# RMS norms of a two-block transformer kernel: sums in four column groups of 128 tokens, root and reciprocal on 128 columns, spread back by a one-row selector product

## The reference, cut to what matters

```python
def rms_norm(x, g):
    xf = x.astype(jnp.float32)
    y = xf * lax.rsqrt(jnp.mean(xf * xf, axis=-1, keepdims=True) + EPS)
    return (y * g.astype(jnp.float32)).astype(x.dtype)
```

## Time and profile before

| | before |
|---|---|
| median of 3 runs | 3803.28 us |
| the profiled execution | 3806.89 us |
| its span in the trace | 3805.1 us |
| mean granted TensorE clock | 0.903 of 2.4 GHz |
| PE busy | 3185.7 us (84%) |
| DVE busy | 1077.3 us (28%) |
| ACT busy | 647.6 us (17%) |

### The profile page before, as it was taken

How to read it: one execution, slowest core, us unless ns; L and a number is a source line. 1 busy time by engine, 2 the same in 40 slices (tenths; PEclk the granted TensorE clock), 3 DMA queues, 4 the chain that set the end, 5 groups by cost and what they waited for, 6 DMA issues and landing times.

```text
span 3805.1 us, 44308 instructions
## 1 busy us (share of the span) xinstructions
PE 3185.7 (84%) x18944; PEld 1617.3 (43%) x18944; DVE 1077.3 (28%) x2009; ACT 647.6 (17%) x1340; POOL 194.5 (5%) x180
## 2 busy tenths in 40 slices
PE   6896679999788888999999976728899989989873
PEld 3552234444333444566666654413344433333331
DVE  3341330000422121145555554331112111111114
ACT  0131100000001222234433442000111101101100
POOL 0000000000000000011111111020000000000001
PEclk9996789999897888999999996759999999999986
DMA  3114212212100000411111100065777899999993
GB/s 144 45 56 174 103 44 78 76 56 88 47 31 18 18 28 28 160 39 44 51 39 39 39 34 2 9 222 234 311 305 314 360 404 379 386 395 385 398 375 149
DMA packets 119322, 581.11 MB, mean 153 GB/s; under 512 B 12806, under 2 KB 24086, under 8 KB 72534
## 3 DMA queue, kind: packets, MB, share of 16 engines
q1 hardware_dynamic: 92274, 531.69, 35.6%
q10 hardware_dynamic: 20436, 24.26, 1.8%
q0 software_dynamic: 6416, 22.32, 1.6%
HBM read 549.76 MB, written 28.47 MB: 152 GB/s over the span
## 4 chain that ended last, share of the span: by engine, by line
PE 73%; DMA 12%; DVE 9%; ACT 3%; issue 2%; POOL 1%; SPq 0%; DVEq 0%; POOLq 0%; ACTq 0%
PE product_banks L768 35%; PE product_banks L1011 12%; DMA space<-in_wgu 8%; PE product_banks L1033 7%; PE score_banks L814 4%; PE score_banks L942 3%; PE turn_bank L799 3%; PE out_bank L836 2%; DVE rstd L1340 1%; DMA space<-in_wt 1%; PE turn_bank L827 1%; PE product_banks L755 1%; DMA y_rows<-zeros 1%; PE turn_bank L1022 1%; DVE space L1544 1%
## 5 line engine op out<-in xcount | busy, mean ns | idle before, releaser
L768 PE MATMUL product_banks<-space 128*128 128x512 f32 (+3 forms) x4064 | 1453.5, 511 | 56.4 <-DVE space L1471 15.3
L768 PEld LDWEIGHTS product_banks<-space 128*128 128x128 f32 (+1 forms) x4064 | 711.5, 193 | 711.5 <-issue 621.3
L1011 PE MATMUL product_banks<-space 128*32 128x512 f32 x5440 | 630.0, 608 | 64.0 <-DMA space<-in_wgu 62.5
L1011 PEld LDWEIGHTS product_banks<-space 128*32 128x32 f32 x5440 | 180.0, 111 | 451.7 <-issue 327.9
L1033 PE MATMUL product_banks<-space,rstd 128*32 128x256 f32 x5440 | 332.3, 399 | 46.4 <-ACT rstd L1275 30.3
L1663 DVE TENSOR_TENSOR sq<-product_banks,space 128x512 f32<-128x512 f32 x85 | 58.8, 692 | 758.4 <-PE product_banks L1011 758.4
L1033 PEld LDWEIGHTS product_banks<-space,rstd 128*32 128x32 f32 x5440 | 207.0, 115 | 152.6 <-issue 83.5
L1118 ACT ACTIVATE space<-product_banks 128x512 f32<-128x512 f32 (+2 forms) x238 | 113.0, 526 | 881.9 <-PE product_banks L768 879.0
L814 PE MATMUL score_banks<-space 64*128 64x256 f32 (+5 forms) x352 | 173.6, 598 | 34.9 <-ACT space L1132 17.9
L799 PE MATMUL turn_bank<-sq,cst 128*128 128x512 f32 (+1 forms) x196 | 107.0, 685 | 112.3 <-DVE sq L1336 112.0
L684 POOL TENSOR_TENSOR space<-space 128x512 f32<-128x512 f32 x112 | 133.8, 1209 | 1180.0 <-ACT space L1214 1087.4
(11 more groups left out here) (241 smaller groups left out, 2154.6 us busy)
## 6 DMA issues: line engine op xcount, KB each, us to landing
space<-in_wgu SPq DMA_DIRECT2D x256, 1024.0 KB, 13.9
space<-in_wdn SPq DMA_DIRECT2D x128, 1024.0 KB, 20.7
space<-in_wt SPq DMA_DIRECT2D x104, 1024.0 KB, 5.4
y_rows<-zeros ACTq DMA_DIRECT2D x2, 6400.0 KB, 27.7
y_rows<-zeros ACTq DMA_DIRECT2D x85, 128.0 KB
space<-in_wt SPq DMA_DIRECT2D x12, 512.0 KB, 4.3
space<-in_wt SPq DMA_DIRECT2D x8, 576.0 KB, 3.8
x<-in_xT SPq DMA_DIRECT2D x1, 2048.0 KB, 15.8
```

Of the source, the lines that this page charges most:

```text
L768: ins = nc.tensor.matmul(bank[0:rows, at:at + cols], lhsT, rhs, start=(i == 0), stop=(i == len(mm) - 1))
L1011: ins = nc.tensor.matmul(bank[ROWS * g:ROWS * g + ROWS, :], xT_[:, k, :], w[:, 512 * g:512 * g + 512], start=(k == 0), stop=(k == DC - 1))
```

## The change

Sums: a chunk's 512 columns are taken as four quarters of 128 tokens, and quarter q is multiplied by 32 columns of ones into PSUM partitions 32q to 32q+31, columns 0 to 127. One 128x512 product becomes four of 32x128 in four column groups of the array. Root: ACT reads the sums straight from PSUM, 128 columns on all partitions, and takes scale and epsilon with it (a new constant `eps`). DVE's mean-plus-epsilon instruction is gone, and its reciprocal is on 128 columns. Spreading: a new PE piece, `norm_spread`, multiplies `rstd` by a matrix that picks row 32q (a column of the identity, broadcast), once for each quarter, and writes the 512 values on all partitions into the PSUM bank `out_bank` (`PO`). The applications read them there. Norms of 256 columns do the same with 64.

```diff
+                    for q in range(4):
+                        ins = nc.tensor.matmul(PT[ROWS * q:ROWS * q + ROWS, 0:w // 4], ones[:, 0:ROWS], sq[:, g % 2, w // 4 * q:w // 4 * (q + 1)],
+                                               start=(c == 0), stop=(c == nch - 1))
+                    ins.then_inc(s_mm, 1)
...
+            def norm_spread(name):
+
+                n = NI[name]
+                w = NORMS[n][3]
+                pe.wait_ge(s_inv, n + 1)
+                for q in range(4):
+                    ins = nc.tensor.matmul(PO[:, w // 4 * q:w // 4 * (q + 1)], ident[:, ROWS * q:ROWS * q + 1].broadcast_to([P, P]),
+                                           rstd[:, 0:w // 4], start=True, stop=True)
+                ins.then_inc(s_rs, 1)
...
             norm("pre_mix")
+            norm_spread("pre_mix")
             norm("mem")
+            norm_spread("mem")
             pe.wait_ge(s_norm, normed("pre_mix", 1))
             products("in1", "pre_mix")
...
                 for d in range(2):
                     fill(2 * d)
-
+                    if n and d == 0:
+                        norm_spread(f"head{n - 1}")
                     pe.wait_ge(s_kd, 2 * n + d + 1)
...
                 norm(f"head{n}")
+            norm_spread("head7")
...
-                act.wait_ge(s_ms, n + 1)
-                nc.scalar.activation(ms[:, 0:w], ms[:, 0:w], F.Sqrt).then_inc(s_rt, 1)
+                _, _, nch, w = NORMS[n]
+                act.wait_ge(s_mm, chunk0[n] + nch)
+                nc.scalar.activation(ms[:, 0:w // 4], PT[:, 0:w // 4], F.Sqrt, bias=const("eps"), scale=1.0 / (P * nch)).then_inc(s_rt, 1)
...
-                dve.wait_ge(s_mm, chunk0[n] + nch)
-                V.tensor_scalar(ms[:, 0:w], PT[:, 0:w], 1.0 / (P * nch), EPS, ALU.mult, ALU.add).then_inc(s_ms, 1)
                 dve.wait_ge(s_rt, n + 1)
-                link(V.reciprocal(rstd[:, 0:w], ms[:, 0:w]))
+                V.reciprocal(rstd[:, 0:w // 4], ms[:, 0:w // 4]).then_inc(s_inv, 1)
+                dve.wait_ge(s_rs, n + 1)
...
-                link(V.scalar_tensor_tensor(osb, osb, vcol("hg_norm_g_2"), rstd[:, :], ALU.mult, ALU.mult))
+                link(V.scalar_tensor_tensor(osb, osb, vcol("hg_norm_g_2"), PO[:, :], ALU.mult, ALU.mult))
```

More of the change, by code:

```diff
@@ L59 @@
           ("more_no", N_MORE), ("token_no", TT), ("group_of", P), ("tie", N_EXP), ("rank_at", N_EXP), ("row_at", N_EXP),
-          ("room_at", N_EXP)]
+          ("room_at", N_EXP), ("eps", 1)]
 CONST_AT = {}
@@ L288, in build @@
         s_mm = sem("squares_summed")
-        s_ms = sem("mean_squares_ready")
         s_rt = sem("roots_ready")
+        s_inv = sem("inverse_roots_ready")
+        s_rs = sem("inverse_roots_spread")
         s_norm = sem("norm_written")
@@ L798, in norm @@
                     pe.wait_ge(s_sq, g + 1)
-                    nc.tensor.matmul(PT[:, 0:w], ones, sq[:, g % 2, 0:w], start=(c == 0), stop=(c == nch - 1)).then_inc(s_mm, 1)
+                    for q in range(4):
[10 more added lines that the diff above has]
+                ins.then_inc(s_rs, 1)
             def rope(r):
@@ L870, in _ @@
             norm("attn")
+            norm_spread("attn")
             norm("conv")
+            norm_spread("conv")
             norm("xattn")
+            norm_spread("xattn")
             pe.wait_ge(s_norm, normed("xattn"))
@@ L875, in _ @@
             norm("post_mix")
+            norm_spread("post_mix")
             norm("pre_mlp")
+            norm_spread("pre_mlp")
             pe.wait_ge(s_norm, normed("pre_mlp", 1))
@@ L881, in _ @@
             norm("post_mlp")
+            norm_spread("post_mlp")
             if stop == "x1":
@@ L884, in _ @@
             norm("mix2")
+            norm_spread("mix2")
             pe.wait_ge(s_norm, normed("mix2", 1))
@@ L887, in _ @@
             norm("ctx")
+            norm_spread("ctx")
             pe.wait_ge(s_norm, normed("ctx"))
@@ L890, in _ @@
             norm("qin")
+            norm_spread("qin")
             norm("ckv_lat")
+            norm_spread("ckv_lat")
             norm("ckv_ctx")
+            norm_spread("ckv_ctx")
             pe.wait_ge(s_evac, stages["in2"][1])
@@ L962, in _ @@
             norm("ffn2")
+            norm_spread("ffn2")
             pe.wait_ge(s_norm, normed("ffn2"))
@@ L1093, in _ @@
             norm("final")
+            norm_spread("final")
         @block.scalar
@@ L1344, in norm_apply @@
                 for c in range(nch):
-                    V.scalar_tensor_tensor(dst[:, c, 0:w], src[:, c, 0:w], gain(c), rstd[:, 0:w], ALU.mult,
+                    V.scalar_tensor_tensor(dst[:, c, 0:w], src[:, c, 0:w], gain(c), PO[:, 0:w], ALU.mult,
                                            ALU.mult).then_inc(s_norm, 1)
@@ L1446, in add_normed @@
                 for c in range(nch):
-                    link(V.scalar_tensor_tensor(src[:, c, :], src[:, c, :], gain(c), rstd[:, :], ALU.mult, ALU.mult))
+                    link(V.scalar_tensor_tensor(src[:, c, :], src[:, c, :], gain(c), PO[:, :], ALU.mult, ALU.mult))
                     link(V.tensor_tensor(x[:, c, :], x[:, c, :], src[:, c, :], ALU.add))
@@ L1780, in constants @@
     put("room_at", np.array([ROWS * n for n in BLOCKS_AT] + [0])[None, :])
+    put("eps", EPS)
     put("token_no", (np.arange(P)[:, None] + P * np.arange(TT)[None, :]))
```

3 lines of the change are left out of this document (1 added, 2 removed).

## The result

The changed kernel takes 3864.71 us (median of 4 runs, 3861.95 to 3873.74) against 3803.78 (4 runs): a ratio of 1.0165, with a 95% interval of 1.0153 to 1.0178. It is 1.6% slower. The profiled execution took 3861.95 us, its span is 3859.9 against 3805.1, its mean granted clock 0.895 against 0.903.

The account below looks back on a forecast made before the run. PE was taken to bound most of the span, plus norms where everything waits. 3806.89 + 120 (heads) - 57 (norms) = 3870 us for a profiled execution, 3.6 above the median, so 3866; range 3840 to 3892, 8 in 10 within 3830 to 3900.

Parts of the forecast that it names:

- DVE waits for a spreading that stands behind the fill, and PE for DVE: Passages into heads 1 to 6: PE's turns start 17.2 us later a head, 103 us in all, bounds 96 to 109.
- The clock after the wait: Heads, after PE's wait: work restarts at the lower clock, losing 2.8 us a head, 17 for six, bounds 0 to 27.
- The eight heads together: Head norms: stall and clock add 120 us for heads 0 to 5; ends of heads 6 and 7 save 4.3.
- The fifteen norms by themselves: Norms with no other work beside them: quicker sums, root and reciprocal save time, within a 57 us total including heads 6 and 7.
- Applications from PSUM at nothing: DVE's applications in the norms: reading the factor from PSUM costs nothing, gain or loss up to 0.05 us each.
- Up to four times for four column tiles: Norm sums on PE: the skill's rule would make a chunk some 0.2 us, not 0.46, the sum about 4 us better.
- The drain at a change of mode: Heads, PE switching between projections and sums: the skill's rule says each tiling switch drains the engine; no size was given.
- the clock stays low: Rival, chance 0.10: in the heads, slow work after each stall costs 10 us a head instead of 2.8; 3909 us.
- The wait is not on PE's path: Rival, chance 0.05: spreading gets ahead of the fill or DVE's 15.97 us is covered; only norms' gain stays, 3746 us.

Follow-up runs that it names:

- e3: Changed kernel with each head's spreading moved on PE from behind all 26 products of the fill to behind the first 4; 3748.77 us, ratio 0.9861.
- e4: Changed kernel plus 16 constant products on PE between the spreading and the turns in heads 1 to 6; 3843.37 us, ratio 1.0109.
- e1: Kernel before, with the new norm in the eight head norms only and the fifteen others old; 3925.13 us, ratio 1.0323.
- e2: Kernel before, with the new norm in the fifteen standalone norms only and the eight head norms old; 3740.08 us, ratio 0.9839.
- e6: Changed kernel with each head's spreading placed on PE ahead of all 26 products of the fill; 3771.56 us, ratio 0.9921.
- e8: e2 plus constant products on PE behind a norm's last chunk and between norms, none between chunks; 3728.48 us, ratio 0.9803.
- e7: e2 plus constant products on PE behind each chunk's sums, behind the last chunk and between norms, final norm excepted; 3742.70 us, ratio 0.9847.

## Why the prediction was right

The predicted time was 3866 us, the measured 3864.7. By its steps:

- *DVE waits for a spreading that stands behind the fill, and PE for DVE.* Right, in its place and its size: 17.2 us a head were forecast, the turns start 17.0 later relative to the fill. The uncovered chain of DVE that head 7 showed before, 15.97 us, was the wait of 15.92 that PE has now. One sign was off: DVE's idle time ahead of L1536 was to be about 18 us and is 20.90. e3 shows that this order is the cause.
- *The clock after the wait.* 2.8 us a head forecast, 2.8 in the profile from turns to L954, and e4 measured 3.6 by keeping PE at work. It was taken as half of the 5.6 us of work after which the clock was back in mix2; in the heads it was back 5.5 us after the start of the turns. The term holds to within a microsecond. 17.0 and 3.6 make 20.6; the traces have 123.0 / 6 = 20.5 a head.
- *The eight heads together.* +120 for heads 0 to 5 and -4.3 for the ends of heads 6 and 7, so +116: the traces have +123.0 and -3.2, e1 has +121.4. Some 4 to 6 us too little.
- *The fifteen norms by themselves.* The -57 holds those 4.3 of heads 6 and 7, so -53 was forecast here. e2 measured -63.6, the traces have -65.0: 11 to 12 us too little. Where the forecast priced norms it was near: mix2 was to take 10.6 and takes 10.0; conv 5.7, and takes 5.6; post_mlp's end 3.3 to 4.4, and it is 3.6 (the pace was forecast at 0.82 a chunk, and is 0.735 in mix2). From attn's first square to ckv_ctx's first application the trace is 41.4 us shorter, for 40 forecast; pre_mix, ffn2 and final save 6.1, 5.1 and 4.7, for 4.8 each. Most of the rest lies elsewhere: from mem's first square to attn's, where a loss of 1 was forecast, it is 3.8 less, and in the experts, from ffn2's first application to final's first square, 4.6 less (1340.1 for 1344.7), though no changed norm stands in them. e1 has the old norms in both stretches, and is 1.7 below the kernel before in the first and 0.8 above in the second; e2 to e6 and e8, with the new norms, take 1335 to 1340 in the second. Why these two are shorter is open.
- *Applications from PSUM at nothing*: right, 748 against 747 to 752 ns.
- *Up to four times for four column tiles* (the Trainium skill, TensorEngine Tiling (Array Packing), Theoretical Speedup): a chunk's eight sum instructions take 0.42 to 0.43 us at full clock, where before two of 128x512 took 1.02. That is 2.4 times, and close to the 0.46 taken from the experts' rows. But where two chunks follow each other the sixteen take 0.64 (963.72 above), so the second adds 0.22, while two of 128x512 add 0.87 in the fill (22.58 us for 52). For the pace the trace agrees with the four times, and with the 0.2 us a chunk that the prediction worked out by them; a chunk that stands alone has some 0.2 us besides, in which its last instructions come through. *The drain at a change of mode* (the Trainium skill, same page, Key Properties): in the heads the sums start at 1661.83, 0.52 us behind the start of the projection instruction ahead of them (1661.31), where these follow each other every 0.43 and the old sum did so too. So 0.1 us is lost there; whether by a drain or because the weights load late, no run tells. In e7, where sums and added products take turns at the lower clock, a chunk takes 1.42 us, and an estimate from the two paces above, at half the clock, gives 0.44 for its sums and 0.54 for its product (160 of 512 columns of twice 0.87); some 0.4 us are left for two changes of form.

Of the rivals, "the clock stays low" (3909) did not happen: it was back 5.5 us after the turns began. "The wait is not on PE's path" (3746) is what e3 built, and it measured 3748.8; that kernel has another order on PE than the one forecast. The total fits better than its terms. For an execution like the profiled one it was 3870, and that came out at 3861.95, 8 us lower: by the traces the heads cost 4 more than forecast, and the norms by themselves gained 12 more. The medians agree better, by 1.3 us, because the changed kernel's profiled execution lies 2.8 below its median while before's lies 3.1 above. That two misses of opposite sign and this came to 1.3 is luck; what the runs bear out is the mechanism, and each of the two parts to within 12 us.

## What to carry to other kernels

When a step is moved from one engine to another, ask where in the new engine's order it will stand, and what the old engine's next dozen instructions were hiding behind. Here a norm that is 1.6 times quicker wherever nothing else runs (15.76 to 10.01 us in mix2) cost 20 us a head where it had cost nothing, and moving four products from behind the last of 26 others to behind the fourth turned +1.6% into -1.4%. A spreading (or any hand-over that is answered later) wants independent work on both sides of it: enough ahead that its input is there, enough behind that what it releases is done before the next wait. And take such a change apart by stage before judging it: 63.6 us of gain lay under 121.4 of loss.

## What the runs showed of the hardware that was not expected

- The four sums of a chunk's pass, one in each column group, ran side by side: in the changed kernel they start 7 ns apart, and the next four 0.11 us later (from 963.72). Eight of them take 0.43 us, or 0.22 behind others of their kind, where the eight of the spreading, with 128 moving columns each as well, take 1.05.
- Added work for the clock's sake is not free below full clock: with products of 160 columns a chunk takes PE 0.83 us at 2.4 GHz (510.37 to 511.20) and 1.42 at 1.2 GHz, where DVE alone sets 0.73, and the clock had fallen all the same. Placed only where PE idled, the same idea was worth 11.6 us of the medians.
- In the changed kernel PE is idle from 1686.5, and the granted clock is 0.99 over 1688 to 1691 and 0.50 from there. In e6 it was 0.54 over 1667 to 1670, a microsecond after PE had taken up work again behind a wait of only 3.58 us.
- The reciprocal's time on DVE goes with its columns: 553 ns at 64 (the three norms of 256 columns in the changed kernel), 953 at 128, 1753 at 256 and 3353 at 512, 6.25 ns a column and 153 besides; the square of 128x512 takes 688. That is why a norm's reciprocal is worth doing on 128 columns at all.
